# Merge of a hybrid decoder layer: gates and w_out by seven block products in place of eight, the branch matmuls of a pair of tiles between the fourth and the fifth product

## The reference, cut to what matters

```python
branch = jnp.einsum('bskw,kwd->bskd', ys, branch_w)
gates = jax.nn.sigmoid(xn @ merge_gate_w + merge_gate_b).reshape(bn, s, N_BRANCH, d)
merged = jnp.sum(gates * branch, axis=2)
return merged @ w_out
```

## Time and profile before

| | us |
|---|---|
| runs before | 2483.79, 2485.73, 2494.85 |
| median | 2485.73 |
| profiled execution, span | 2490.9 |
| of it mixer, up to the merge's first matmul | 459.2 |
| of it merge | 1114 |
| of it routing, experts and final norm | 918 |

### The profile page before, as it was taken

One profiled execution on the slowest core, in us unless ns is written; L12 is line 12 of the kernel. 1 busy time (PEld: TensorE's weight loads), 2 busy tenths in 40 slices (PEclk: granted clock), 3 DMA queues, 4 the chain that ended last, 5 costly groups with the idle time before them and its releaser, 6 DMA issues. The chain is left out here.

```text
span 2490.9 us, 33940 instructions
## 1 busy us (share of the span) xinstructions
PE 2344.6 (94%) x11340; PEld 1842.1 (74%) x11341; DVE 1374.7 (55%) x2038; ACT 1107.2 (44%) x1410; POOL 675.7 (27%) x516
## 2 busy tenths in 40 slices
PE   6999989999999999999999999499999999999991
PEld 5777768788888888888888887377667776677771
DVE  7697767644443444444443444656555655557565
ACT  4534333233333333333333332367556665567663
POOL 3831101100000000000000000277555756558771
PEclk9999999999999999999999999699999999999995
DMA  7964846443463335433453323398778888789987
GB/s 216 354 245 161 317 155 203 125 129 96 131 215 126 99 114 188 151 120 95 152 192 93 95 85 126 137 336 318 269 260 290 300 293 288 261 306 365 326 289 287
DMA packets 314109, 517.42 MB, mean 208 GB/s; under 512 B 35420, under 2 KB 213856, under 8 KB 297632
## 3 DMA queue, kind: packets, MB, share of 16 engines
q1 hardware_dynamic: 297520, 458.44, 52.4%
q0 software_dynamic: 16496, 57.74, 9.3%
HBM read 431.17 MB, written 84.94 MB: 207 GB/s over the span
## 5 line engine op out<-in xcount | busy, mean ns | idle before, releaser
L1555 PE MATMUL mrgps<-xn_hi,w_hi 128*128 128x512 f32 x1016 | 397.0, 391 | 0.0
L1555 PE MATMUL mrgps<-xn_lo,w_hi 128*128 128x512 f32 x1016 | 395.4, 389 | 0.0
L1555 PE MATMUL mrgps<-xn_hi,w_lo 128*128 128x512 f32 x1016 | 395.4, 389 | 0.0
L2088 POOL TENSOR_TENSOR w_lo<-w_raw,w_hi 128x1024 fp32r<-128x1024 f32 x128 | 343.6, 2835 | 0.0
L2252 PE MATMUL exps<-w_hi,x_room 128*128 128x512 f32 x1024 | 331.5, 400 | 3.5 <-DVEq L2423 3.0
L1476 ACT ACTIVATE gt<-mrgps,mb 128x512 f32<-128x512 f32 x128 | 88.3, 690 | 507.1 <-PE mrgps L1555 500.5
L1827 POOL MEMSET x_ident<- 128x128 f32 x1 | 0.2, 200 | 1110.8 <-POOLq L1271 1110.8
L2083 DVE TENSOR_TENSOR w_lo<-w_raw,w_hi 128x2048 fp32r<-128x2048 f32 x127 | 285.4, 2306 | 0.0
L1693 DVE SCALAR_TENSOR_TENSOR tmp<-gt,mrgps 128x512 f32<-128x512 f32 x96 | 66.0, 687 | 384.9 <-PE mrgps L1555 384.9
L2073 ACT ACTIVATE w_hi<-w_raw 128x2048 fp32r<-128x2048 f32 x128 | 239.1, 1921 | 9.1 <-DMA w_raw<-in_expert_w_dram 9.0
L2252 PEld LDWEIGHTS exps<-w_hi,x_room 128*128 128x128 f32 x1024 | 193.4, 189 | 63.4 <-issue 16.9
(11 more groups left out here) (449 smaller groups left out, 4150.2 us busy)
## 6 DMA issues: line engine op xcount, KB each, us to landing
w_raw<-in_expert_w_dram SPq DMA_DIRECT2D x192, 1024.0 KB, 8.8
w_raw<-in_merge_gate_w_dram SPq DMA_DIRECT2D x128, 512.0 KB, 4.0
win_hi<-w_in_parts SPq DMA_DIRECT2D x42, 512.0 KB, 4.1
win_lo<-w_in_parts SPq DMA_DIRECT2D x42, 512.0 KB, 5.6
w_raw<-in_branch_w_dram SPq DMA_DIRECT2D x128, 128.0 KB, 4.1
wout<-in_w_out_dram SPq DMA_DIRECT2D x64, 256.0 KB, 4.7
w_raw<-in_x_dram SPq DMA_DIRECT2D x16, 512.0 KB, 7.8
branch_rows<-in_x_dram SPq DMA_DIRECT2D x16, 512.0 KB, 5.8
```

Of the source, the lines that this page charges most:

```text
L1555: last = pe.matmul(bank[:], w[:, u % 2, kk], x, start=(kk == w_tiles[0] and j == 0), stop=(kk == w_tiles[-1] and j == 2))
L2088: eng.tensor_tensor(self.lo2[:, f], self.raw2[:, f], self.hi2[:, f].bitcast(F32), ALU.subtract).then_inc(self.split2, 1)
```

## The change

`merge_branches` is written anew. It treats the tokens in two pairs of 512-token tiles, the chunks (3, 2) first, then (0, 1). For each pair, each pair of channel blocks `dp` and each branch `k` there is one group `q`, 32 in all: gate weights of 1024 by 256 (2 by 2 blocks of 512 by 128) times `xn` of 1024 by 1024 (2 by 2 blocks of 512 by 512). Four corners, `11`, `12`, `21`, `22` (channel block, token tile), are wanted. The first two groups (`PLAIN`) compute them by eight block products of 12 matmuls. From the third on, and for w_out, it is the scheme with seven: sums `s1` to `s4` of weight blocks, sums `t1` to `t4` of `xn` blocks, and sums of products.

```diff
+    FAST = (("11", "11", "a"), ("s2", "t2", "b"), ("12", "21", "a"), ("s1", "t1", "c"), ("s3", "t3", "d"), ("s4", "22", "c"), ("22", "t4", "d"))
+    FOUR = (("11", "11", "a"), ("12", "21", "a"), ("21", "11", "d"), ("22", "21", "d"),
+            ("11", "12", "c"), ("12", "22", "c"), ("21", "12", "b"), ("22", "22", "b"))
```

Each triple is a product: weight item, `xn` block, PSUM bank. Products 1 and 3 share bank a, 4 and 6 bank c, 5 and 7 bank d. TensorE's part, with the waits of a product that goes on in a bank already begun:

```diff
+            def product(q, i):
...
+                low.reached(pe, (q, item))
+                if start and q:
+                    bank_free(pe, bk, q - 1)
+                if not start and kind(q) != "plain":
+                    if bk == "a":
+                        p1_set.reached(pe, q)
+                    else:
+                        comb.reached(pe, (q, "z" if bk == "c" else "22"))
...
+            for q in range(PLAIN, NA):
+                for i in range(4):
+                    product(q, i)
+                branches(q)
+                for i in (4, 5, 6):
+                    product(q, i)
```

`branches(q)` is 24 matmuls, six for each corner, into four banks of their own. The sums of products are VectorE's, `u2` and `z` being tiles in SBUF:

```diff
+            def second(q):
...
+                comb.done(dve.tensor_tensor(u2[:], first_part[:], bank["b"][:], ALU.add), (q, "u2"))
+            def third(q):
...
+                comb.done(dve.tensor_tensor(z[:], u2[:], bank["c"][:], ALU.add), (q, "z"))
+            def corner(q, c):
+
+                prod.reached(dve, (q, ends["gate"][c]))
+                comb.reached(dve, (q, "z"))
+                b = bank["c" if c == "12" else "d"]
+                if c == "22":
+                    comb.done(dve.tensor_tensor(z[:], z[:], b[:], ALU.add), (q, c))
+                else:
+                    comb.done(dve.tensor_tensor(b[:], b[:], u2[:], ALU.add), (q, c))
```

`first_part` is ScalarE's copy of bank a after product 1 (`first_copy`, which marks `p1_set`). The orders of the two engines in a gate group:

```diff
+            for q in range(PLAIN, NA):
...
+                first_copy(q)
+                part_high(q, "s4")
...
+                part_high(q, "22")
+                tanh(q, "11")
...
+                for i in ("11", "s2", "12"):
+                    part_high(q + 1, i)
+                if q + 1 < NA:
+                    wb_high(q + 1)
+                tanh(q, "22")
+                tanh(q, "12")
+                part_high(q + 1, "s1")
+                if q + 1 < NA:
+                    rows_high(q + 1)
+                part_high(q + 1, "s3")
+                tanh(q, "21")
...
+                second(q)
+                part_low(q, "22")
+                third(q)
...
+                corner(q, "22")
+                for i in ("11", "s2", "12"):
+                    part_low(q + 1, i)
+                gate(q, "11")
+                if q + 1 < NA:
+                    wb_low(q + 1)
+                gate(q, "22")
+                corner(q, "12")
+                gate(q, "12")
+                part_low(q + 1, "s1")
+                if q + 1 < NA:
+                    rows_low(q + 1)
+                part_low(q + 1, "s3")
+                corner(q, "21")
+                gate(q, "21")
```

```diff
+            def refill(q, i):
+
+                b = products[kind(q)][i][1]
+                prod.reached(sp, (q, i))
...
+                    sp.dma_start(X[:, kept[b]].bitcast(F32), dram["wout_blocks"][blocks.index(b)]).then_inc(block_in[b], 16)
```

`merged` goes to DRAM and comes back as the weight side of eight row groups (256 tokens each, FAST again, w_out blocks as the other side). In a row group VectorE first makes the previous group's norms (`norms`), and SP's order is:

```diff
+            for q in range(NA, NQ):
+                if q > NA:
+                    store_h(q - 1, 0)
+                    store_h(q - 1, 1)
+                if q + 1 < NQ:
+                    load_raw(q + 1)
+                if q > NA:
+                    store_xn(q - 1, 0)
+                    store_xn(q - 1, 1)
+                    load_rows(q)
```

In the mixer, the last chunk of the branches is now stored as the others are, and the merge's first weights are those of one group:

```diff
-            dr.filled(sp, ("pool", CH - 1, 1))
-            load_merge_weights(sp, io, w_raw, merge_w_in, NBR - 1, 0)
+            store(1, CH - 1, yb_full, pl)
+            store(3, CH - 1, yd_full, lg)
+            store(0, CH - 1, ya_full, ya)
```

More of the change, by code:

```diff
@@ L1285, in merge_branches @@
[L1285 to L1291, removed]
+            return ctx.enter_context(nc.semaphore("mg_" + name))
+        ps = [ctx.enter_context(nc.psum_tensor(f"mrgps{i}", [P, TC], F32)) for i in range(8)]
+        bank = dict(zip("abcd", ps))
@@ L1540, in _ @@
+            r = NQ - 1 - NA
+            turn(r, 0)
+            logitsT(r, 0)
+            turn(r, 1)
+            logitsT(r, 1)
         @block.tensor
         def _(pe):
-            def first_product(bank, tiles):
-                pe.wait_ge(w_hi_set, 1)
-                for kk, parts in enumerate(tiles):
-                    for j, x in enumerate(parts):
-                        pe.matmul(bank[:], w_hi[:, 0, kk], x, start=(kk + j == 0), stop=False)
-                pe.wait_ge(w_split, 1)
-                for kk, (x, _) in enumerate(tiles):
-                    last = pe.matmul(bank[:], w_lo[:, 0, kk], x, start=False, stop=(kk == KD - 1))
-                return last
@@ new lines, in branches @@
+            def branches(q):
+                b_low.reached(pe, q)
+                for c in corners[kind(q)]:
+                    n, t = where[c]
+                    y_low.reached(pe, (q, t))
+                    if q:
+                        gated.reached(pe, (q - 1, c))
+                    for j in range(2):
+                        for s, (w, y) in enumerate(((wb[0], ys_hi), (wb[0], ys_lo), (wb[1], ys_hi))):
+                            last = pe.matmul(bbank[c][:], w[:, j, n * P:(n + 1) * P], y[:, t, j], start=(j + s == 0), stop=(j == 1 and s == 2))
+                    branch.done(last, (q, c))
@@ new lines, in turn @@
+            def turn(r, t):
+                pe.wait_ge(n_full, 2 * r + t + 1)
+                if r + t == 0:
+                    gated.reached(pe, (NA - 1, corners["gate"][-1]))
+                for h in range(2):
+                    if r + t:
+                        pe.wait_ge(t_free, 2 * (2 * r + t) + h - 1)
+                    for kk in range(4):
+                        last = pe.transpose(tbank[h][:, kk * P:(kk + 1) * P], xn[:, t, (4 * h + kk) * P:(4 * h + kk + 1) * P], ident[:])
+                    last.then_inc(t_full, 1)
@@ L1662, in _ @@
+            r = NQ - 1 - NA
+            turn(r, 0)
+            rout(r, 0)
+            turn(r, 1)
+            back(r, 0)
+            rout(r, 1)
+            back(r, 1)
         @block.vector
```

1071 lines of the change are left out of this document (649 added, 422 removed).

## The result

The changed kernel takes 2631.9 us (median of 4 runs, 2625.1 to 2634.9), against 2485.0 for the kernel before (4 runs on the same chip): a ratio of 1.058, 95% interval 1.055 to 1.060. The profiled span is 2629.8, 138.9 above that of before.

A forecast was written before the change was run, and what follows sets the result against it. The prediction took TensorE's matmul stream to bound the merge; -103 + 82 + 45 + 8 + 9 + 20 + 20 = +81 on the profiled span of 2490.9 gave 2572, or 2567 us as measured by runs, range 2500 to 2635.

The forecast's parts named there:

- matmuls: Gate and row groups: seven products instead of eight remove 456 matmuls of 0.2267 us each, -103 us.
- loop stalls: Gate groups: TensorE waits for ScalarE's bank a copy before the third product, 3.2 us (1.2 behind k = 0), +82 us.
- clock: Gate groups: three in four of 23 stalls drop TensorE to half clock, 2.6 us each, +45 us.
- pieces: Low parts for the next pair's blocks in 16 groups: hidden behind VectorE's waits; uncovered, under 0.6 us each.
- start: Merge start: VectorE waits 7 to 8 us for mb behind four transfers, and the mixer ends later: +8 us.
- pair change: Where the pair of tiles changes: seven block loads of 2.1 MB and weights outlast their cover, +9 us.
- change to w_out: Between gate and row groups: block transfers and VectorE's wait for the router's weights hold TensorE, +20 us.
- row groups: w_out: late x rows make a loop of 28.3 against 25.5 us, 7 x 2.8 = +20 us.
- Rival 3: Gate groups: every loop stall pays the clock fall, 60 us in place of 45, total 2582; chance 0.20.
- Two things cost nothing while their cover holds: Gate groups: GpSimd's four sums (5.7 us) and the pieces of the next pair's blocks stay hidden, no cost.
- Rival 4: Whole merge: all returns at 1.2 GHz (+99 for 45) and transfers near 300 GB/s, total 2640; chance 0.09.
- Rival 2: Gate groups: VectorE and ScalarE pass the chain in under 11.1 us, no stalls or clock loss, total 2440; chance 0.11.

The follow-up runs named there:

- run 10: run 9 plus 13 matmuls that do not count in TensorE's stall (6 behind a group with k = 0): 2547.5 us, 1.024.
- run 9: The changed kernel with GpSimd's steps on the next blocks' pieces cut to 8 of 256 columns, blocks mostly not computed: 2576.9 us, 1.036; last copy 10.6 us earlier.
- run 3: The changed kernel with VectorE's low part of s3 made behind corner 21, not ahead of it: 2601.6 us, 1.045.
- run 4: The changed kernel with the gate bias as the first transfer of the merge, not the fifth: 2629.0 us, 1.057.
- run 8: run 4, run 6 and run 7 together, plus router-weights wait moved to the second row group, that group's weights asked for ahead: 2613.0 us, 1.050.
- run 6: The changed kernel with the bank a copy directly behind corner 12's tanh and GpSimd's pieces held back until that copy: 2622.7 us, 1.054.
- run 7: The changed kernel, row groups only: x rows asked for first, first tile's transposes copied ahead of the high part awaiting weights: 2632.0 us, 1.056.
- run 12: run 1 with run 4's bias, run 8's w_out step, run 7's orders extended to both transposes and first logits, corner 22 before low parts: 2574.8 us, 1.034.
- run 1: The changed kernel with ScalarE's copy of the next group's bank a ahead of corner 21's tanh in gate groups: 2593.6 us, 1.042.

## Why the prediction was right in kind and short in size

The bound moved from TensorE's stream to a loop of waits through VectorE and ScalarE, for the reason given and at the price given. The terms, in us; those of the gate groups go by the 29 periods from the copy of group 2 (547.13) to that of 31 (1416.00), 868.9 us where 29 x 24.5 = 710.5 is matmuls alone:

| term | predicted | found | from |
|---|---|---|---|
| matmuls | -103 | -103 | 108 a window at full clock in 24.7 |
| loop stalls | +82 | +87 | run 10: 22 x 3.4 + 7 x 1.8 |
| clock | +45 | +26 | run 10 against 9 |
| pieces | 0 | +26 | run 9: 10.6; second pair of run 10: 235.7 against 220.0 (6 x 27.9 + 2 x 26.3) |
| start | +8 | +28 | 547.1, where 459.2 + 252 x 0.2267 + 0.4 is due; before lost 2.4 there too (16 matmuls in its first 6.0 us) |
| pair change | +9 | +14 | run 10: 33.1 + 32.6 + 30.3, where 27.9 + 26.3 + 27.9 is due |
| change to w_out | +20 | +21 | 26.9 + 44.4, where 24.5 + 25.5 is due |
| row groups | +20 | +33 | 6 x 31.05, where 25.5 is due |

They add up to +132 of 138.9; 7 are not assigned. Against the sum of 81 that is 51 more: 26 of pieces, 20 of the start, 13 of row groups, 11 of the stalls, the pair change and w_out, less 19 of the clock.

- **A new loop of waits**: right. The gap of 3.2 is 3.17 in the trace, and it follows a step taken out of the chain by the same 0.60 (run 3). The 1.2 behind k = 0 is 1.6; three adds of 0.60 are 1.8 and not 2.0, which gives 1.4.
- **The clock**: the share was right (three in four; 11 of 14), the size was not. I priced a fall at 2.6 us from one stretch of 5.6 us at 0.50; in a group without pieces it is 29.54 less 27.92, 1.6. The 6 us behind most falls hold 19 or 20 matmuls, where 26 or 27 pass at full clock; the 13 in 5.6 us that I took for the rule are its long case (two of the 11). The prediction also says that the trace before has no gap of 1 to 3 us at full clock ahead of large matmuls: it has, 1.87 us at 314.42, with a clock of 1.00 in the 6 us behind. Rival 3 (every stall pays) fell by the 3 of 14, and more by run 3, where most gaps of 2.57 pay nothing. The case of the Trainium skill cited for it (TensorE: Matmul & The Clock Gate, "HAM oscillation — how this bites in real kernels"), with waits of some 3 to 5 us, drops the clock in every turn; here 11 of 14 stalls of 3.2 us did, and 5 of 12 that were shorter by 0.6.
- **"Two things cost nothing while their cover holds"** is the step that failed. The pieces were costed as VectorE's own low parts, under 0.6 each, behind the wait for product 5. Two things went past that: GpSimd's steps arrive with their load at the end of a group, beside VectorE's low parts, and hold one for 2.83 us; and in the second pair the fourth room is free only when a store has landed, so that three low parts come after product 5, and beside GpSimd's sums. Of the 26 us, 10.6 were taken away by run 9; the other 16 are a difference from the bare loop, with these rows as the likely cause. The Trainium skill (SBUF — State Buffer, "SBUF: two separate sides") says that GpSimd and a VectorE step with two SBUF inputs take their shared ports in turn, each for the whole instruction. The rows at 667 us agree: 2.83 beside 2.48. I had priced VectorE's steps by rows in which GpSimd was idle (POOL 0.00).
- **The start**: a mis-sized term. The wait for mb was 13.1 and not 7 to 8, and I had not followed the second group's weights behind the same 4 MB (491.6), which run 4 shows to take over when the bias is first. The clock was 0.85 over the first 102 us.
- **The change to w_out**: right to 1 us, but partly by luck: the blamed wait, held to cost most of the 20, was worth 8 when it was moved together with the next weights (run 8 against 6).
- **Row groups**: the loop named (x rows asked for late, VectorE 10 us idle) is there, but with it a second one, ScalarE's copies behind a high part that waits for weights. That holds TensorE for 3.8 a group. Removing the x-row link and half of the other gave nothing (run 7), more of both 1.7 a group (run 12).
- **Rival 4** (everything pays, 2640) comes nearer in number than the forecast, but not in kind: the clock took 26 us and not 99, and pieces, start and row groups made up the rest. That the measured time is in the range owes something to luck: the clock was 19 too dear where the pieces were 26 too cheap.
- **Rival 2** (matmul-bound, 24.5) is what run 1 comes near to in the groups without pieces: 25.4 to 26.8. That the copy could stand ahead of the tanh was in the prediction; that this alone would not pay in the other half of the groups was not.

## What to carry to other kernels

A scheme with fewer matmuls gives its saving only as long as no engine waits in a ring: add up the chain from a product to the next product that needs its bank, queue order included, and compare it with the matmuls in between; here that sum gave the period to 0.2 us (27.7 for 27.9, at full clock and without pieces). Then price steps of VectorE that read two SBUF operands beside everything GpSimd does in the same stretch, and look at when loads and stores will release them, not only at how long they take. When one link of such a ring is cut, look for the next in the trace before adding up gains: of 135, 129 and 32 us expected from runs 1, 6 and 7, 38, 9 and 0 came.

## What the runs showed of the hardware

- A 128 x 512 subtraction of VectorE with both inputs in SBUF, 0.69 us alone, took 2.83 beside a GpSimd step of 128 x 1024 (2.48), and 1.22 beside its shorter ones; corner 21, with an input in PSUM, stayed at 0.68 beside one of 1.05 (the change, 667 to 674 us).
- The granted clock fell, in most cases for some 3 us, behind 11 of 14 stalls of 3.17 to 3.21 us (the change), 5 of 12 of 2.56 to 2.58 (run 3), and none of 4 of 1.6 (the change). One fall cost a group 1.6 us.
- Filling the stall with matmuls that count for nothing took 26.5 us off a kernel whose useful work was the same (run 10 against 9): the time TensorE idled was not the only price of idling.
